# Half of the cached key pages turned in 32x32 blocks by VectorE, from a load in another layout

## The reference, cut to what matters

```
pages of sequence s:  page_table[s, 0..15], a page is 128 keys x (8 heads x 64) float32 = 256 KB
z[h, t, key] = (q[t, h] . k[key, h]) / sqrt(64) + bias_h        for each of the 4 new rows t
a[h, t, key] = sigmoid(z) * product over later keys of (1 - sigmoid(z))
out[h, t]    = sum over key of a[h, t, key] * v[key, h]
```

## Time and profile before

| what | value |
|---|---|
| runs | 2372.18, 2375.03, 2370.04 us; median 2372.18 |
| profiled execution: span from first to last instruction | 2370.8 us |
| profiled execution: time of its own | none is given beside the span; the median of the runs is 1.4 us above the span |
| PE busy over the span | 2289.0 us, 97% |
| PE weight loads | 2033.8 us, 86% |
| DVE / ACT / POOL busy | 1621.7 (68%) / 1081.2 (46%) / 49.0 (2%) us |
| DMA | 292275 packets, 328.41 MB, mean 139 GB/s |
| page loads | 128 of `in_cache_k` and 128 of `in_cache_v`, 256.0 KB each, median 4.1 and 4.2 us to landing |

### The profile page before, as it was taken

One profiled execution on the slowest core, in us unless ns is written; L12 is line 12 of the kernel. 1 busy time (PEld: TensorE's weight loads), 2 busy tenths in 40 slices (PEclk: granted clock), 3 DMA queues, 4 the chain that ended last, 5 costly groups with the idle time before them and its releaser, 6 DMA issues. The chain is left out here.

```text
span 2370.8 us, 47763 instructions
## 1 busy us (share of the span) xinstructions
PE 2289.0 (97%) x18824; PEld 2033.8 (86%) x18824; DVE 1621.7 (68%) x2754; ACT 1081.2 (46%) x1979; POOL 49.0 (2%) x108
## 2 busy tenths in 40 slices
PE   7999999999999999999969999899999999999998
PEld 7999999987879888888858875577999999997776
DVE  7766766657885486666546797657676766765886
ACT  7322222234563677566745565435522222223453
POOL 0000000000000100000010000010000000000000
PEclk9999999999999999999979999999999999999999
DMA  5343333365463222122138878723143343436454
GB/s 160 103 144 109 117 121 98 118 215 190 131 199 96 63 61 76 54 59 62 48 130 292 263 244 314 244 101 125 44 156 120 100 135 102 133 126 231 141 165 153
DMA packets 292275, 328.41 MB, mean 139 GB/s; under 512 B 18810, under 2 KB 200058, under 8 KB 292113
## 3 DMA queue, kind: packets, MB, share of 16 engines
q1 hardware_dynamic: 292112, 326.16, 42.7%
HBM read 254.63 MB, written 71.47 MB: 138 GB/s over the span
## 5 line engine op out<-in xcount | busy, mean ns | idle before, releaser
L1227 PE MATMUL a_q<-a_uh,a_p_hi 128*128 128x352 f32 x672 | 236.4, 352 | 0.0
L1229 PE MATMUL a_q<-a_uh,a_p_lo 128*128 128x352 f32 x672 | 216.3, 322 | 0.0
L1228 PE MATMUL a_q<-a_ul,a_p_hi 128*128 128x352 f32 x672 | 215.9, 321 | 0.0
L1227 PEld LDWEIGHTS a_q<-a_uh,a_p_hi 128*128 128x128 f32 x672 | 126.6, 188 | 21.3 <-issue 18.8
L1228 PEld LDWEIGHTS a_q<-a_ul,a_p_hi 128*128 128x128 f32 x672 | 127.1, 189 | 0.1
L1229 PEld LDWEIGHTS a_q<-a_uh,a_p_lo 128*128 128x128 f32 x672 | 126.1, 188 | 0.0
L884 PE MATMUL c_q<-c_b_hi,c_a_hi 128*128 128x512 f32 x264 | 104.7, 397 | 2.4 <-DVE c_b_lo L785 1.3
L884 PE MATMUL a_q<-a_b_hi,a_a_hi 128*128 128x512 f32 x264 | 103.6, 392 | 2.1 <-DVE a_a_lo L783 1.9
L885 PE MATMUL c_q<-c_b_hi,c_a_lo 128*128 128x512 f32 x264 | 104.1, 394 | 0.0
L886 PE MATMUL c_q<-c_b_lo,c_a_hi 128*128 128x512 f32 x264 | 103.8, 393 | 0.0
L886 PE MATMUL a_q<-a_b_lo,a_a_hi 128*128 128x512 f32 x264 | 102.8, 389 | 0.0
(11 more groups left out here) (736 smaller groups left out, 7742.7 us busy)
## 6 DMA issues: line engine op xcount, KB each, us to landing
b_page<-in_cache_k SPq DMA_DIRECT2D x128, 256.0 KB, 4.1
b_page<-in_cache_v SPq DMA_DIRECT2D x128, 256.0 KB, 4.2
a_w_raw<-in_ffn_gu SPq DMA_DIRECT2D x44, 512.0 KB, 5.2
c_w_raw<-in_ffn_gu SPq DMA_DIRECT2D x44, 512.0 KB, 5.0
a_a_raw<-hid_rows SPq DMA_DIRECT2D x66, 256.0 KB, 2.7
c_a_raw<-hid_rows SPq DMA_DIRECT2D x66, 256.0 KB, 2.7
a_p_raw<-in_w_in SPq DMA_DIRECT2D x28, 512.0 KB, 4.1
a_raw_d<-in_ffn_d SPq DMA_DIRECT2D x11, 1024.0 KB, 5.2
```

Source lines behind the costliest of these rows:

```text
L1227: nc.tensor.matmul(self.pm[at % 2][:, 0:TB], wh, self.uh[t][:, c], start=(c == 0), stop=False)
L1228: nc.tensor.matmul(self.pm[at % 2][:, 0:TB], wh, self.ul[t][:, c], start=False, stop=False)
L1229: mm = nc.tensor.matmul(self.pm[at % 2][:, 0:TB], wl, self.uh[t][:, c], start=False, stop=(c == KC - 1))
```

## The change

Pages b = 0 and 2 stay as they were. Pages b = 1 and 3 of a key round (64 of the 128 key pages) go another way:

- Load: each page is issued as four DMAs. The i-th takes channels 128i to 128i+127 to partitions 32i to 32i+31; partition 32i+t holds keys 4t to 4t+3, a run of 128 channels (512 bytes) each. The 2 KB runs become four runs of 512 bytes.
- Transpose: one `nc.vector.transpose` of 128x512 takes the place of four PE transposes and one PSUM copy. It turns each 32x32 block; the channels end on partitions 32i + d, the keys in the order (s, t).
- Scores: the moving operand of b = 1, 3 is read with a step of 128 elements between neighbouring keys (`"p s t -> p t s"`), and their channels lie in another order on the partitions. So `qb` is filled separately for even and odd b, from a second load `qs_b` in the new order, and the new keys get a second load `ks_b`.
- Waits: DVE waits for the page itself; SP frees a slot when PE has turned the even pages and DVE the odd ones; PE waits for `qb` only at its first scores.

```diff
-        qs, ks = s.sb("qs", [P, 4, T_S]), s.sb("ks", [P, 4, T_S])
+        qs, ks, qs_b, ks_b = (s.sb(n, [P, 4, T_S]) for n in ("qs", "ks", "qs_b", "ks_b"))
...
+        def page_count(n):
+            rounds = n // SLOTS + 1
+            blocked = min(rounds, len(KEY_ROUNDS) // SLOTS)
+            return 160 * blocked + 64 * (rounds - blocked)
...
             sp.dma_start(qs[:], q_cols.rearrange("c p n -> p c n")).then_inc(E("q_cols_in"), 16)
+            for i in range(4):
+                sp.dma_start(qs_b[rows_in(i)], q_cols[i].rearrange("(c r) n -> r c n", r=R)).then_inc(E("q_cols_in"), 16)
             sp.dma_start(ks[:], k_cols.rearrange("c p n -> p c n")).then_inc(E("small_in"), 16)
+            for i in range(4):
+                sp.dma_start(ks_b[rows_in(i)], k_cols[i].rearrange("(c r) n -> r c n", r=R)).then_inc(E("small_in"), 16)
...
-                        sp.wait_ge(E("k_turned1"), 2 * old + 2)
+                        sp.wait_ge(E("k_turned0"), 2 * old + 2)
+                        sp.wait_ge(E("k_copied1"), 2 * old + 2)
...
-                        sp.dma_start(page[:, n % SLOTS, b:b + 1, :], src.rearrange("g p n -> p g n")).then_inc(E(f"page_in{n % SLOTS}"), 16)
+                        if keys and b % 2 == 1:
+                            for i in range(4):
+                                sp.dma_start(page[rows_in(i), n % SLOTS, b].rearrange("t (s d) -> t s d", s=4),
+                                             src[:, :, i * P:(i + 1) * P].rearrange("g (t s) d -> t (g s) d", s=4)).then_inc(E(f"page_in{n % SLOTS}"), 16)
+                        else:
+                            sp.dma_start(page[:, n % SLOTS, b:b + 1, :], src.rearrange("g p n -> p g n")).then_inc(E(f"page_in{n % SLOTS}"), 16)
...
-                            pe.wait_ge(E(f"page_in{n % SLOTS}"), 64 * (n // SLOTS) + 64)
-                        for e in range(2):
-                            b = 2 * half + e
-                            q = 4 * n + b - 3
-                            at_least(pe, E(f"k_copied{q % 2}"), q // 2 + 1)
-                            for c in range(4):
-                                mm = nc.tensor.transpose(pk[(4 * n + b) % 3][:, c], page[:, n % SLOTS, b, c * P:(c + 1) * P], ident[:])
-                            mm.then_inc(E(f"k_turned{e}"), 1)
+                            pe.wait_ge(E(f"page_in{n % SLOTS}"), page_count(n))
+                        at = 2 * n + half
+                        at_least(pe, E("k_copied0"), at - 2)
+                        for c in range(4):
+                            mm = nc.tensor.transpose(pk[at % 3][:, c], page[:, n % SLOTS, 2 * half, c * P:(c + 1) * P], ident[:])
+                        mm.then_inc(E("k_turned0"), 1)
+
+            def keys_of(n, b, c):
+                if b % 2 == 0:
+                    return k_turned[n % 2][:, b, c]
+                return k_turned[n % 2][:, b, :, rows_in(c)].rearrange("p s t -> p t s")
...
-                        dve.wait_ge(E("k_turned1"), 2 * n + half + 1)
-                        nc.vector.tensor_copy(k_turned[n % 2][:, 2 * half + 1], pk[(4 * n + 2 * half + 1) % 3][:]).then_inc(E("k_copied1"), 1)
+                        if half == 0:
+                            dve.wait_ge(E(f"page_in{n % SLOTS}"), page_count(n))
+                        nc.vector.transpose(k_turned[n % 2][:, 2 * half + 1].rearrange("p c n -> p (c n)"),
+                                            page[:, n % SLOTS, 2 * half + 1]).then_inc(E("k_copied1"), 1)
...
-            pe.wait_ge(E("small_in"), 48)
+            pe.wait_ge(E("small_in"), 112)
...
-            pe.wait_ge(E("q_ready"), G)
-            pe.wait_ge(E("masks_out"), 1)
...
-            dve.wait_ge(E("q_cols_in"), 16)
+            dve.wait_ge(E("q_cols_in"), 80)
             for gi in range(G):
                 for h in range(H_SB):
-                    c, e = h // 2, h % 2
-                    src = qs[e * DH:(e + 1) * DH, c, 16 * gi:16 * gi + 16].rearrange("p (b q) -> p b q", q=L_S)
-                    step = nc.vector.tensor_copy(qb[e * DH:(e + 1) * DH, gi, c, :, L_S * h:L_S * h + L_S], src)
+                    c, e, to = h // 2, h % 2, slice(L_S * h, L_S * h + L_S)
+                    src = qs[e * DH:(e + 1) * DH, c, 16 * gi:16 * gi + 16].rearrange("p (b o q) -> p b o q", o=2, q=L_S)
+                    nc.vector.tensor_copy(qb[e * DH:(e + 1) * DH, gi, c, :, to].rearrange("p (b o) q -> p b o q", o=2)[:, :, 0], src[:, :, 0])
+                    k, pair = rows_in(c), slice(2 * e, 2 * e + 2)
+                    src = qs_b[k, pair, 16 * gi:16 * gi + 16].rearrange("p c (b o q) -> p c b o q", o=2, q=L_S)
+                    step = nc.vector.tensor_copy(qb[k, gi, pair, :, to].rearrange("p c (b o) q -> p c b o q", o=2)[:, :, :, 1], src[:, :, :, 1])
                 step.then_inc(E("q_ready"), 1)
```

More of the change, by code:

```diff
@@ L2720, in scores @@
                     at_least(pe, E("z_out"), r - 1)
+                    if p == 0:
+                        pe.wait_ge(E("q_ready"), gi + 1)
+                    if r == 0:
+                        pe.wait_ge(E("masks_out"), 1)
                     if p < PAGES:
@@ L2723, in scores @@
                             pe.wait_ge(E(f"k_copied{e}"), 2 * (PAGES * gi + p) + 2)
-                        products(flat(pz[r % 2])[:, 0:P], gi, lambda b, c: k_turned[(PAGES * gi + p) % 2][:, b, c])
+                        products(flat(pz[r % 2])[:, 0:P], gi, lambda b, c: keys_of(PAGES * gi + p, b, c))
                     else:
-                        products(flat(pz[r % 2])[:, 0:T_S], gi, lambda b, c: ks[:, c])
+                        products(flat(pz[r % 2])[:, 0:T_S], gi, lambda b, c: (ks, ks_b)[b % 2][:, c])
             def values():
@@ L2749, in values @@
                 yield value_time(G, 0) + PE_AT["values"][2]
-                pe.wait_ge(E("k_copied1"), 2 * len(KEY_ROUNDS))
+                pe.wait_ge(E("k_copied0"), 2 * len(KEY_ROUNDS))
                 for gi in range(G):
@@ L2873, in key_copies @@
                         act.wait_ge(E("k_turned0"), 2 * n + half + 1)
-                        nc.scalar.activation(k_turned[n % 2][:, 2 * half], pk[(4 * n + 2 * half) % 3][:], ACT.Copy).then_inc(E("k_copied0"), 1)
+                        nc.scalar.activation(k_turned[n % 2][:, 2 * half], pk[(2 * n + half) % 3][:], ACT.Copy).then_inc(E("k_copied0"), 1)
             def weigh():
```

## The result

| | before | after |
|---|---|---|
| median of the runs | 2373.2 us (4 runs, 2370.0 to 2375.0) | 2491.9 us (4 runs, 2487.3 to 2493.4) |
| span of the profiled execution | 2370.8 us | 2488.8 us |

The change makes the kernel slower: ratio 1.0498, 95% interval 1.0485 to 1.0512. The forecast was 2416; +118.7 us came where +43.8 was forecast, and 2491.9 lies outside the range of 2385 to 2444.

What follows compares the result with a forecast made beforehand. TensorE bound the key part before, SP's issuing after: 1232.0 + 187.2 + 5.4 put the first value page at 1424.6, scores ended 43.9 us later, span 2370.8 became 2414.7, median 2416; range 2385 to 2444.

Steps and rivals of the forecast that it cites:

- the term of SP's issuing: Key part: SP needs 5.85 us a round, 187 us for 32 rounds where 140 were, and so binds.
- What binds: Key part after the change: SP's issuing at 5.85 us a round, where PE needs 3.4; SP never waits for slots.
- The start: Before the key pages: eight more small loads at 0.45 each, first page 3.6 us later; PE's first piece 6.7 later, hidden.
- I take 0.56: SP's step from one split DMA to the next: 0.52 of a page DMA plus 0.05 for three dimensions.
- 0.45 to 0.60 for a split DMA: Bounds of SP's step per split DMA, giving 2388 us at 0.45 and 2426 at 0.60.
- 5.85: SP's key round in us: 2 x 0.52 for whole pages, 8 x 0.56 for split DMAs, 0.33 for page numbers.
- The lead that SP had: End of the key part: of the 56 us that SP falls behind, 12 are paid by its lead.
- PE, -34.1 us hidden: Key part: 256 of 512 PE transposes go, 34.1 us or 1.07 a round, hidden under SP's issuing.
- rival (1): Faster: SP keeps up, split DMAs under 0.39 us apart; 2361 or about 2345, with doubled scores 2379; chance of faster 0.08.
- DVE's transpose, taken at 0.7: Key part: each 128x512 DVE transpose costs 0.7 us, near the copy it replaces, so nothing gained or lost.
- DMA, 140 us hidden: Key part: 512-byte runs add 15.6 us of DMA engine time, 140 us in all, hidden under SP's 187.
- Rival (2), the clock: Slower: in the key part PE's clock falls to 1.2 GHz, up to 2446 us; clock or chain on top 0.14.

Runs made afterwards that it cites:

- x5: The changed kernel with key 32s+t, not 4t+s, on partition 32i+t, run s, so scores read contiguous columns: 2427.5 us, ratio 1.0228.
- x10: The changed kernel with the first DMA of each odd key page cut in two, three of every four keys and the fourth: 2510.8 us (one run).
- x3: The changed kernel with odd key pages loaded whole as before, its compute unchanged: 2375.2 us, ratio 1.0007.
- x2: The kernel before with each odd key page loaded as four DMAs of 32 whole 2 KB rows: 2426.0 us, ratio 1.0218.
- x6: x5 with each of an odd page's four DMAs writing all 128 partitions with one 512-byte run: 2508.9 us, ratio 1.0570.
- x8: The changed kernel with each odd key page loaded by one DMA, source order i, key, channel: 2520.7 us, ratio 1.0612.
- x12: The kernel before with each odd key page's single DMA of 2 KB rows taken as 4 x 32: 2470.4 us, ratio 1.0411.
- x9: x8 with the scores reading contiguous columns and writing every fourth column of PSUM: 2525.7 us, ratio 1.0633.
- x11: x5 for page b = 3 only, the other three loaded whole and transposed on PE: 2388.8 us, ratio 1.0072.

## Why the prediction was wrong

It had the mechanism and the sign, and the term of SP's issuing too small.

- **What binds: right.** SP never waited for a slot, PE waited for the DMA of the page at its transposes, the value part stayed 130.5 us, the DMA share was 0.55.
- **The start: right in kind.** The first page went out 5.5 us later, not 3.6. The eight loads cost 3.8; the stage had begun 1.8 us later. DVE wrote `qb` until 1236.3 and PE's first transposes came at 1242.85, hidden as said (SP issued the third round from 1249.02). The 32 copies took 6.7 us, not 9.8.
- **The step that failed: "I take 0.56", and its bounds "0.45 to 0.60 for a split DMA".** The step was 0.75 us. I had built it from a 0.33 to 0.39 us instruction and 0.19 of register work. The register work was 0.19 (0.75 - 0.56). The instruction was 0.56, because source and destination rows don't match (x5, x10: 0.32 when they do). That is 8 x 0.19 x 32 = 48.6 us. The nearest rows were loads of another shape. What was needed was the price of a DMA whose two sides cut differently.
- **The rest.** The undisturbed round was 7.57 and not 5.85 + 1.52 = 7.37: 0.2 x 32 = 6.4 us for reading the page numbers and for a whole page's 0.64 instead of 0.52. Instructions that stall now and then, and so the round of 8.17, make the last 14: 261.3 = 32 x 7.57 + 5.4 for the nine other issues + 13.7. The sum had no such term. Together 48.6 + 6.4 + 13.7 = 68.7, the difference between 261.3 and the 192.6 forecast. The lead that SP had paid 9.8, not 12.
- **PE, -34.1 us hidden: half true.** 256 transposes did go, but the scores nearly doubled and took the same back (x3: 32.0 us less, 31.1 more). The text had that only inside rival (1) and without a row; it would have decided if SP had kept pace, 2375 in x3 where the rival said 2379.
- **DVE's transpose, taken at 0.7: right**, 0.688 us.
- **DMA, 140 us hidden: right in effect.** 0.55 x 262.8 = 145 us, if the share is taken as it stands.
- **Rival (1), faster:** it needed a step under 0.39 us, and the cheapest seen was 0.50, in x5, at 2427. **Rival (2), the clock:** it fell to 0.79 in the key part and cost nothing, since PE, at 166 of 263 us, waited for pages all the same.

## What to carry to other kernels

Count the issue steps of the queue before you split a transfer, and price a step by a row whose two sides cut alike or unlike as yours do: 0.50 us against 0.75 for the same 64 KB here, which over 256 DMAs is most of what the prediction missed. If a layout must change the order, choose the one whose source shape follows the destination's (here key 32s+t for 4t+s): it gave 64 of the 119 us back and, with the scores' read changed to match, cured their stride as well. A relief of the binding engine has to be netted against what the new layout does to the next reader: in x3 32 us of transposes went and 31 came back in the scores.

## What the runs showed of the hardware that was not expected

- A DMA instruction on SP's queue took 0.32 to 0.38 us where the two sides have like rows, with 32 to 128 pieces (whole pages, x2, x5, x10), and 0.55 to 0.61 where they don't, with 128 or 512 (the change, x6, x8, x12). That unlike outermost sizes decide is read from these cases; the mechanism behind it is not shown.
- One DMA with an outermost size of 4 held up the next one to 1.5 us (2 KB rows) or 2.7 (512-byte runs), and cost 99 and 147 us of the run, though a key round had no more DMA instructions than in the kernel before. In stretches where it alone moved data, the share of the 16 DMA engines was 0.26 and 0.29, about that of four.
- GpSimd's instruction for a part was 0.548 us where SP's was 0.317.
- Scores that read fp32 at a 512-byte step took about twice as long at a granted clock of 1.00 (2.03 us for 32 records, half of them strided, against 1.08), and little longer at 0.50 (x8 2.03, x9 1.94): the strided ones hardly gain from the higher clock. Those that write fp32 to PSUM at a 16-byte step took no longer (1.08).
- VectorE's fp32 transpose of 128x512 in 32x32 blocks took 0.688 us, as long as the copy of that size from PSUM, and only 2.2 times the 128x128 one of 0.312.
- Still open: the stalls of single issues. After undisturbed rounds, the nine other issues and waits for slots are taken off, about 0.4 us a round are left in x11 and 0.5 to 0.6 in x5 (6.18 a round, 5.4 to 5.5 undisturbed), at DMA shares of 0.91 and 0.77. No run took them apart.
